# Projections on high and low halves, the modulation rows in the weights' ring, and one sequence for the fourth layer's attentions

## The chip, the cores and the metric

The kernel runs on one NeuronCore of a Trainium2 chip. The metric is the device time of one execution in microseconds (us). All data are float32; "fp32r" in a row is the matmul's reduced form of float32 operands.

## The reference

A sequence of 256 tokens of width 1024 goes through four layers. The first block has two layers (gated linear attention and a spatial gating unit, an output projection, cross attention to a memory, 16 experts in 4 groups); the second block has two layers with adaptive norms (the third: sparse "nsa" and block "moba" attention; the fourth: latent "mla" and sliding-window "swa" attention), each again with 16 experts. The adaptive norms take their scales, shifts and gates from a vector c:

```python
for layer in range(DEPTH):
    shift_m, scale_m, gate_m, shift_f, scale_f, gate_f = adaln(c, ada_w[layer], ada_b[layer])
    h = rmsnorm(x, norm_mix[layer]) * (1.0 + scale_m) + shift_m
    # even layer: nsa and moba; odd layer: mla and swa; both start from h @ w_in
    x = x + gate_m * mix.astype(x.dtype)
    h = rmsnorm(x, norm_ffn[layer]) * (1.0 + scale_f) + shift_f
    x = x + gate_f * grouped_moe_2(h, router_w, router_b, ...)
return rmsnorm(x, final_norm)
```

c times ada_w is 2 x 6144 numbers from 50 MB of weights; the projections and experts read 500 MB.

## The kernel before

**Weights.** All weights of the projections and experts come in pieces of 2 MB (128 x 4096) through `ring`, four slots. SyncE issues the loads in one order (L2210): load m waits on `halves_done`, which TensorE raises by two when it starts the piece after the one it gives back, and lands in slot m % 4. A first-block layer has 15 pieces before its experts (q with k, v, r, sv, u, xk0, xk1, out0, out1, xv0, xq0, xq1, xv1, xo0, xo1), the third layer 10, the fourth 6; the experts have 48 per layer.

**Projections.** `natural` keeps x stationary and moves 512 weight columns; `transposed` keeps 128 weight columns and moves x's 256 tokens. Both are plain float32 products of `product` (line 654 of every row: the helper `mm`); the profile shows a plain product as two TensorE records. x comes transposed (`turn`, L684), drained by ScalarE and VectorE in turn (`turned`, `modulated`, L1512, L1870).

**Experts.** The same ring, but each piece in halves: ScalarE writes the high part of a half to `hi_ring` (four half slots, L1155), VectorE writes what is left to `ring_parts` in the piece's place (L1494), and TensorE adds three products, high-high, high-low, low-high. One half later each half is given back. A branch after the loop (L873, L884) recomputes groups with more than 128 tokens; it runs in the third layer alone. Around the attention units the engines follow one list in a fixed order: scores, exponentials, transposed probabilities three steps apart.

**Modulation.** GpSimd loads the rows of ada_w, 48 loads of 1 MB, into `hi_ring` while that is free; VectorE multiplies each row with silu(c) and sums it (`modulation`, L1839, 96 rows) at places of the first two layers chosen by ADA_PLAN (3, 7, 1, 3, 7, 3 loads). GpSimd's next load waits on `ada_summed`.

**Order.** Each engine's stream is written out by hand. `first_layer` (TensorE, L902) runs q, k, alow, v, z, r, sv, rem, dec, u, kv, mix, xk0, o, xk1, turn0, out, xv0, turn1, xq, attention with xv1 in it, xo, turn2, router, experts. In the fourth layer TensorE runs c, the latents' norm and their up projection, mla's attention, then sq and sk, then swa's attention.

## Time and profile before

| | us |
|---|---|
| median of 3 runs (2514.18 to 2517.14) | 2515.72 |
| profiled execution | 2515.05 |
| its span | 2512.9 |
| projections of the second layer, first product to last add | 642.8 to 890.6 |
| experts of the second layer | 934.5 to 1245 |
| third layer: projections, then attention | 1270.7 to 1377.3, to 1458 |
| fourth layer: projections and attentions | 1994.6 to 2097.3 |
| TensorE, VectorE, ScalarE, GpSimd busy | 2192, 1504, 1084, 89 |

A timeline row gives the start of a run of like instructions, its length, engine, line, operation, output and input, shape and count; in brackets the idle time before it and what ended that. The granted clock of TensorE is a share of 2.4 GHz.

### The profile page before, as it was taken

The numbers are of one execution on the slowest core, as the hardware profiler recorded it, in microseconds if no ns is written. First come the engines' busy times: TensorE is split into PE (matmuls) and PEld (weight loads), VectorE is DVE, ScalarE is ACT, GpSimd is POOL, SyncE is SP. The second block draws the span as 40 slices with busy tenths as digits, with TensorE's granted clock in tenths as the row PEclk, the third lists the DMA queues.
The fourth block names the chain that finished last, engine by engine and source line by source line (L and its number), as shares of the span: only waits on it lengthen the run. The fifth ranks groups of instructions, "written<-read, shape, count | busy, mean of one in ns | idle before, by whom it ended". The sixth has DMA issues, their size and how long they took to land.

```text
span 2512.9 us, 25829 instructions
## 1 busy us (share of the span) xinstructions
...
## 2 busy tenths in 40 slices
...
GB/s 408 285 228 199 84 327 329 285 342 321 275 236 256 159 78 335 342 292 335 268 167 134 1 67 170 334 299 333 314 260 258 71 101 67 137 316 330 303 318 125
DMA packets 48680, 596.26 MB, mean 237 GB/s; under 512 B 5200, under 2 KB 7248, under 8 KB 8784
## 3 DMA queue, kind: packets, MB, share of 16 engines
...
## 4 chain that ended last, share of the span: by engine, by line
PE 64%; issue 21%; DVE 7%; ACT 3%; DMA 3%; POOL 1%; DVEq 0%; ACTq 0%; POOLq 0%
PE bank L654 58%; PE bank L684 2%; PE bank L873 2%; DMA hi_ring<-in_ada 1%; DMA x<-in_x_in 1%; PE bank L884 1%; DVE ring_parts L1494 1%; POOL small L2141 1%; DVE work L1494 1%; ACT hi_ring_parts L1155 1%; ACT mix L1155 0%; ACT work L1155 0%; DVE mix L1569 0%; DVE hi_ring L1839 0%; DVE work_parts L1494 0%
## 5 line engine op out<-in xcount | busy, mean ns | idle before, releaser
L1494 DVE TENSOR_TENSOR ring_parts<-ring,hi_ring_parts 128x2048 fp32r<-128x2048 f32 x384 | 860.6, 2285 | 112.8 <-ACT hi_ring_parts L1155 112.7
L1155 ACT ACTIVATE hi_ring_parts<-ring 128x2048 fp32r<-128x2048 f32 x384 | 722.7, 1913 | 144.3 <-PE bank L654 112.7
L654 PE MATMUL bank<-hi_ring_parts,xT_parts 128*128 128x512 f32 x1024 | 340.5, 405 | 48.6 <-DVE ring_parts L1494 48.6
L1155 ACT ACTIVATE work<-bank 128x512 f32<-128x512 f32 (+6 forms) x215 | 113.6, 531 | 612.3 <-PE bank L654 493.9
L654 PE MATMUL bank<-hi_ring_parts,work_parts 128*128 128x512 f32 x1024 | 328.5, 392 | 24.7 <-DVE work_parts L1494 24.7
L654 PE MATMUL bank<-hi_ring_parts,oT_parts 128*128 128x512 f32 x1024 | 331.3, 394 | 4.8 <-DVE ring_parts L1494 4.8
L654 PEld LDWEIGHTS bank<-hi_ring_parts,xT_parts 128*128 128x128 f32 x1024 | 199.1, 194 | 94.6 <-DVE ring_parts L1494 52.7
L654 PEld LDWEIGHTS bank<-hi_ring_parts,work_parts 128*128 128x128 f32 x1024 | 192.2, 188 | 69.9 <-issue 30.5
L654 PEld LDWEIGHTS bank<-hi_ring_parts,oT_parts 128*128 128x128 f32 x1024 | 192.3, 188 | 48.1 <-DVE ring_parts L1494 8.6
L654 PE MATMUL bank<-ring_parts,xT_parts 128*128 128x512 f32 x512 | 204.9, 400 | 0.0
L654 PE MATMUL bank<-ring_parts,oT_parts 128*128 128x512 f32 x512 | 199.5, 390 | 0.0
L654 PE MATMUL bank<-ring_parts,work_parts 128*128 128x512 f32 x512 | 199.5, 390 | 0.0
L1155 ACT ACTIVATE work_parts<-bank 128x512 fp32r<-128x512 f32 (+1 forms) x116 | 64.5, 560 | 251.7 <-PE bank L684 218.1
L654 PE MATMUL bank<-ring,oT 128*128 128x512 f32 x384 | 166.1, 593 | 4.6 <-DVE oT L1599 2.3
L654 PE MATMUL bank<-ring,xT 128*128 128x512 f32 (+3 forms) x480 | 162.9, 498 | 1.6 <-DVE xT L1870 1.6
L654 PE MATMUL bank<-xT,ring 128*128 128x256 f32 x656 | 148.2, 388 | 16.4 <-DMA xT<-in_xT_in 11.3
L654 PEld LDWEIGHTS bank<-xT,ring 128*128 128x128 f32 x656 | 127.2, 195 | 35.4 <-DMA xT<-in_xT_in 11.3
L654 PE MATMUL bank<-work 128*128 128x128 f32 (+4 forms) x712 | 119.6, 313 | 17.9 <-ACT work L1155 17.8
L654 PEld LDWEIGHTS bank<-ring,oT 128*128 128x128 f32 x384 | 72.5, 190 | 94.3 <-issue 94.3
L654 PEld LDWEIGHTS bank<-ring,xT 128*128 128x128 f32 x480 | 83.6, 190 | 76.4 <-issue 74.6
L1839 DVE CUSTOM_DVE_ANT_0 hi_ring<-hi_ring,silu_row 128x1024 f32<-128x1024 f32 x96 | 112.4, 1221 | 26.9 <-DMA hi_ring<-in_ada 25.7
L654 PEld LDWEIGHTS bank<-work 128*128 128x128 f32 (+1 forms) x712 | 104.1, 208 | 30.4 <-issue 19.3
...
## 6 DMA issues: line engine op xcount, KB each, us to landing
...
```

Source lines behind the costliest of these rows:

```text
L654: ins = nc.tensor.matmul(o, lhsT, rhs, start=start, stop=stop)
L684: ins = nc.tensor.transpose(bank[0:rows, c0:c1], src, ident[0:k, 0:k])
L873: ins = nc.tensor.matmul(psum[j][:, :], xg[0][:, c, :], w[:, c, :], start=c == 0, stop=c == DC - 1)
L884: ins = nc.tensor.matmul(psum[3 + n][:, :], ehT_plain[:, 0, j, :], w[:, j, n * 512:(n + 1) * 512], start=j == 0, stop=j == HC - 1)
L1155: return nc.scalar.activation(o, i, f, **kw)
L1494: return v.tensor_tensor(o, a, b, op)
L1839: v.tensor_tensor_reduce(out=here[:, r, :], in0=here[:, r, :], in1=silu_row, scale=1.0, scalar=0.0, op0=ALU.mult, op1=ALU.add, accum_out=s ...
L2141: nc.gpsimd.tensor_tensor(stat_out, stat_in, cs("half"), ALU.pow).then_inc(rstd_ready, 1)
```

## The change

Four things change. **Three passes:** all projections but xk0, xk1, xv0, xv1, e.ck, e.cv, o.up and the second block's out pieces are split like the experts' pieces and done as three fp32r passes per product; their x is split too (`first_x`, `second_x`, `first_o`, on ScalarE and VectorE, in place of one copy each). Each split stands at a fixed place in ScalarE's and VectorE's streams, and TensorE waits for both halves. **The modulation rows** become 24 pieces of 2 MB in the ring, at fixed places (FIRST_LAYER has nine, EVEN_LAYER six); their slots are given back by `ada_summed`. GpSimd loads none. Part of the sums moves to the third layer. **The gates' 24 columns** join piece e.kw. **Fourth layer:** sq and sk come before the latents' transposes, and mla and swa form one list of attention units. The low-rate product alow comes first in the second layer.

```diff
+FIRST_LAYER = ("q/ v/ a r/ a sv/ a a u/ xk0 xk1 out0/ out1/ a xv0 xq0/ xq1/ a xv1 xo0/ a xo1/ a a").split()
+EVEN_LAYER = "q/ c/ a kw/ a mq/ a ck a cv a mk/ a mv/ out0 out1".split()
+ODD_LAYER = "c/ sq/ sk/ up out0 out1".split()
+LINEAR = {"0": FIRST_LAYER, "1": FIRST_LAYER, "e": EVEN_LAYER, "o": ODD_LAYER}
...
+        class Part:
+
+
+            def __init__(self, name, h):
+                m, n = PIECE_AT[name]
+                self.slot, self.full = m % RING, 16 * (m // RING + 1)
+                self.n = n + h + 1
+                self.free = SPLIT_HALVES[self.n - 1 - HI_RING] + 1 if self.n > HI_RING else 0
+                self.raw = ring[:, self.slot, h * HALF:(h + 1) * HALF]
+                self.hi = hi_ring[:, (self.n - 1) % HI_RING, :]
+                self.lo = ring_parts[:, self.slot, h * HALF:(h + 1) * HALF]
+
...
+            def split_piece(name):
+
+                m, n = PIECE_AT[name]
+                assert PIECES[m] == ("pe", taken[0]), name
+                taken[0] += 1
+                pe.wait_ge(lo_ready, n + 2)
+                release[0] += owed[0]
+                owed[0] = 2
+                parts = [Part(name, h) for h in range(2)]
+                return [[side(p).rearrange("p (c n) -> p c n", c=DC // 2) for p in parts]
+                        for side in (lambda p: p.hi, lambda p: p.lo)]
+
             def mm(o, lhsT, rhs, start, stop):
...
+            def moving(x_, w, T, at, n):
+
+                hi, lo = (lambda c, k=k: w[k][c // 4][:, c % 4, at:at + n] for k in range(2))
+                t = slice(T * P, (T + 1) * P)
+                return [pair for c in range(DC) for pair in ((x_[0][:, c, t], hi(c)), (x_[0][:, c, t], lo(c)),
+                                                             (x_[1][:, c, t], hi(c)))]
+
+            def still(x_, w, m):
+
+                hi, lo = (lambda c, k=k: w[k][c // 4][:, c % 4, m * P:(m + 1) * P] for k in range(2))
+                return [pair for c in range(DC) for pair in ((hi(c), x_[0][:, c, :]), (lo(c), x_[0][:, c, :]),
+                                                             (hi(c), x_[1][:, c, :]))]
+
+            def natural3(name, w, T, x_, at=0, n=512):
...
+                tg = f"{l}"
+                parts = 4 * l
+
+                def low_rate():
+                    wl = pr("w_alow", 2, DC * 16)[:, l, :].rearrange("p (c n) -> p c n", c=DC)
+                    product(f"{tg}.alow", [(0, S, GATE_RANK, [(wl[:, c, :], plain_xT[:, c, :]) for c in range(DC)])])
+
+                if l:
                     for q in range(DC // 2):
                         ready(f"{l - 1}.turn3.{q}")
-                tg = f"{l}"
-                w = columns(piece())
-                transposed(f"{tg}.q", [lambda c, m=m: w[:, c, m * P:(m + 1) * P] for m in range(2)])
-                product(f"{tg}.k", [(T * 256, (T + 1) * 256, P, [(xT[:, c, T * P:(T + 1) * P], w[:, c, 256:512])
-                                                               for c in range(DC)]) for T in range(NT)])
+                    low_rate()
+                w = split_piece(f"{tg}.q")
+                for q in range(DC // 2):
+                    pe.wait_ge(parts_lo, parts + q + 1)
+                transposed3(f"{tg}.q", w, first_x, range(2))
+                both3(f"{tg}.k", w, first_x, 256)
                 if l == 0:
                     pe.wait_ge(setup_loaded, 32)
-                wl = pr("w_alow", 2, DC * 16)[:, l, :].rearrange("p (c n) -> p c n", c=DC)
-                product(f"{tg}.alow", [(0, S, GATE_RANK, [(wl[:, c, :], xT[:, c, :]) for c in range(DC)])])
-                w = columns(piece())
-                for T in range(NT):
-                    natural(f"{tg}.v.{T}", T, lambda c: w[:, c, :])
+                    low_rate()
+
+                def projected(n):
+                    w = split_piece(f"{tg}.{n}")
+                    for T in range(NT):
+                        natural3(f"{tg}.{n}.{T}", w, T, first_x)
+
+                projected("v")
 
                 def memory_values(q):
-                    w = columns(piece())
+                    w = columns(piece(f"{tg}.xv{q}"))
                     for T in range(NT):
...
             normed("o.turn0", 8)
-            w = columns(piece())
+            w = split_piece("o.c")
+            parts_ready(12)
             for T in range(NT):
-                natural(f"o.c.{T}", T, lambda c: w[:, c, 0:448], n=448)
+                natural3(f"o.c.{T}", w, T, second_x, n=448)
+            w = split_piece("o.sq")
+            for j in range(2):
+                transposed3(f"o.sq.{j}", w, second_x, (2 * j, 2 * j + 1))
+            w = split_piece("o.sk")
+            transposed3("o.sk", w, second_x, (0,))
+            both3("o.sv", w, second_x, 0)
             pe.wait_ge(lat_ready, 1)
...
+            attention(numbered(mla_units(), ATT["mla"]) + numbered(swa_units(), ATT["swa"]))
...
+            def split(name):
+
+                for h in range(2):
+                    part = Part(name, h)
+                    act.wait_ge(slot_full[part.slot], part.full)
+                    if part.free:
+                        act.wait_ge(halves_done, part.free)
+                    fn(part.hi, part.raw, ACT.Identity).then_inc(hi_ready, 1)
+
...
+            def x_hi(dest, src, q, tag=None):
+
+                if tag:
+                    banks.wait_drained(act, f"{tag}.{q}")
+                fn(dest[:, 2 * q:2 * q + 2, :], src[:, 2 * q:2 * q + 2, :], ACT.Identity).then_inc(parts_hi, 1)
+
...
-                    turned(f"{l - 1}.turn3")
+                    split(f"{tg}.q")
+                    turned(f"{l - 1}.turn3", plain_xT)
+                    for q in range(DC // 2):
+                        x_hi(first_x[0], plain_xT, q, f"{l - 1}.turn3")
+                split(f"{tg}.v")
+                if l:
+                    whole(alow[0:GATE_RANK, :], f"{tg}.alow")
                 whole(gqT, f"{tg}.q", scale=0.125)
-                whole(alow[0:GATE_RANK, :], f"{tg}.alow")
+                if l == 0:
+                    whole(alow[0:GATE_RANK, :], f"{tg}.alow")
+                split(f"{tg}.r")
                 for T in range(NT):
                     whole(gv[:, T, :], f"{tg}.v.{T}")
                 act.wait_ge(gla_abs, l + 1)
                 step(fn(gE, gE, ACT.Exp, scale=-1.0))
                 fn(gE, gE, ACT.Ln, bias=1.0).then_inc(gla_log, 1)
+                split(f"{tg}.sv")
                 for T in range(NT):
                     whole(gr[:, T, :], f"{tg}.r.{T}", ACT.Silu)
+                split(f"{tg}.u")
                 for T in range(NT):
                     whole(sv[:, T, :], f"{tg}.sv.{T}", ACT.Gelu_apprx_tanh)
                 whole(gE, f"{tg}.rem", ACT.Exp)
                 whole(decay, f"{tg}.dec", ACT.Exp)
+                split(f"{tg}.out0")
                 for T in range(NT):
                     whole(su[:, T, :], f"{tg}.u.{T}", ACT.Gelu_apprx_tanh)
                 for j in range(4):
                     whole(xkT[:, 2 * j:2 * j + 2, :], f"{tg}.xk.{j}")
-                for q in (0, 2):
-                    whole(oT[:, 2 * q:2 * q + 2, :], f"{tg}.turn0.{q}")
+                    if j == 1:
+                        split(f"{tg}.out1")
+                turned_hi(f"{tg}.turn0", first_o[0])
+                split(f"{tg}.xq0")
+                split(f"{tg}.xq1")
 
                 def memory_values(q):
                     for T in range(NT):
                         whole(xv[:, T, q * 512:(q + 1) * 512], f"{tg}.xv.{T}.{q}")
 
                 memory_values(0)
-                turned(f"{tg}.turn1")
+                turned_hi(f"{tg}.turn1", first_x[0])
                 for j in range(4):
                     whole(xqT[:, 2 * j:2 * j + 2, :], f"{tg}.xq.{j}", scale=0.0625)
-                attention(numbered(cross_units(f"{tg}.x"), ATT[f"{tg}.x"]), lambda: memory_values(1))
+                    if j == 1:
+                        split(f"{tg}.xo0")
+
+                def last_values():
+                    split(f"{tg}.xo1")
+                    memory_values(1)
+
+                attention(numbered(cross_units(f"{tg}.x"), ATT[f"{tg}.x"]), last_values)
                 if l == 0:
...
+            def modulation(pieces=1):
+
+                for _ in range(pieces):
+                    n = adas[0]
+                    adas[0] += 1
+                    m = PIECE_AT["a", n]
+                    dve.wait_ge(slot_full[m % RING], 16 * (m // RING + 1))
+                    rows = ring[:, m % RING, :].rearrange("p (r k) -> p r k", r=ADA_EACH)
                     for r in range(ADA_EACH):
-                        k = adas[0] - ADA_COLS * l
-                        adas[0] += 1
-                        v.tensor_tensor_reduce(out=here[:, r, :], in0=here[:, r, :], in1=silu_row, scale=1.0, scalar=0.0,
-                                               op0=ALU.mult, op1=ALU.add,
-                                               accum_out=sm("modc", 2, ADA_COLS)[:, l, k:k + 1]).then_inc(ada_summed, 1)
+                        k = n * ADA_EACH + r
+                        v.tensor_tensor_reduce(out=rows[:, r, :], in0=rows[:, r, :], in1=silu_row, scale=1.0, scalar=0.0,
+                                               op0=ALU.mult, op1=ALU.add, accum_out=sm("modc")[:, k:k + 1]) \
+                            .then_inc(ada_summed, 1)
...
-                    turned(f"{l - 1}.turn3")
+                    split(f"{tg}.q")
+                    turned(f"{l - 1}.turn3", plain_xT)
+                    x_lo(first_x, plain_xT)
+                split(f"{tg}.v")
                 p_ = bank(f"{tg}.k")
                 drained(f"{tg}.k", v.tensor_copy(gk, p_[:, :].rearrange("p (t n) -> p t n", t=2)))
-                modulation(l, ADA_PLAN["key"])
+                split(f"{tg}.r")
+                modulation()
 
                 p_ = bank(f"{tg}.z")
                 z = p_[:, :].rearrange("p (t n) -> p t n", t=2)
@@ -1925,7 +2130,9 @@
                 tell(gla_abs)
                 dve.wait_ge(gla_log, l + 1)
                 tt(gg, gg, gE, ALU.subtract).then_inc(gla_g, 1)
-                modulation(l, ADA_PLAN["gate"])
+                split(f"{tg}.sv")
+                modulation(3)
+                split(f"{tg}.u")
                 banks.wait_drained(dve, f"{tg}.rem")
                 for c in range(NCHUNK):
                     T = c // 2
@@ -1951,6 +2158,7 @@
                 tt(sv, sv, mixv[:, 2:3, :].broadcast_to([P, NT, 512]), ALU.add).then_inc(sgu_ready, 1)
                 dve.wait_ge(sgu_ready, l + 1)
 
+                split(f"{tg}.out0")
                 banks.wait_drained(dve, f"{tg}.dec")
...
-                turned(f"{tg}.turn0", oT)
-                residual(f"{tg}.out", l, ADA_PLAN["out"])
+                turned_lo(f"{tg}.turn0", first_o)
+                split(f"{tg}.out1")
+                residual(f"{tg}.out", l, (0, 1, 0, 0), f"{tg}.xq0")
                 layer_norm(x)
                 tell_x()
-                turned(f"{tg}.turn1")
-                modulation(l, ADA_PLAN["query"])
+                turned_lo(f"{tg}.turn1", first_x)
+                split(f"{tg}.xq1")
+                modulation()
+                split(f"{tg}.xo0")
                 attention(numbered(cross_units(f"{tg}.x"), ATT[f"{tg}.x"]))
-                residual(f"{tg}.xo", l, ADA_PLAN["xo"])
+                split(f"{tg}.xo1")
+                residual(f"{tg}.xo", l, (1, 1, 1, 0))
                 layer_norm(x)
                 tell_x()
                 turned(f"{tg}.turn2")
                 route(tg, "b_router", True)
                 step(v.tensor_scalar(mix[:, :, :], x[:, :, :], ALPHA, None, ALU.mult))
-                modulation_bias(l)
                 dve.wait_ge(rows_out, 128)
                 experts(f"{tg}.moe")
                 layer_norm(mix)
...
+            modulation_bias(0)
+            split("e.q")
+            adaptive_norm("e.turn0", 0, pr("norm_mix")[:, 0:8], 8, 0, second_x)
+
+            split("e.c")
+            modulation()
+            split("e.kw")
+            modulation()
             p_ = bank("e.c")
             for j, pos in enumerate(("pos_k", "pos_v")):
...
+            modulation_bias(1)
+            split("o.c")
+            adaptive_norm("o.turn0", 1, pr("norm_mix")[:, 8:16], 8, 0, second_x)
+            split("o.sq")
             banks.wait_drained(dve, "o.c.0")
             banks.wait_drained(dve, "o.c.1")
...
+            def freed(m):
+                kind, n = PIECES[m]
+                if kind == "pe":
+                    sp.wait_ge(halves_done, 2 * n + 2)
+                else:
+                    sp.wait_ge(ada_summed, ADA_EACH * (n + 1))
+
+            m = 0
+            for tag, linear in LINEAR.items():
+                for _ in range(len(linear) + RING):
+                    if m == 1:
+                        sp.wait_ge(xT_loaded, 16)
+                    if m == 2:
+                        sp.wait_ge(setup_loaded, 32)
+                    if m >= RING:
+                        freed(m - RING)
+                    load(m)
+                    m += 1
+                with sp.Fori(1, NMOE // RING) as g:
+                    for j in range(RING):
+                        sp.wait_ge(halves_done, g * (2 * RING) + (2 * (MOE_USER[tag] + j - RING) + 2))
```

## Rows read from the trace of the kernel before

**Rows 1.** The page: the chain that ended last, by engine.
```profile
PE 64%; issue 21%; DVE 7%; ACT 3%; DMA 3%; POOL 1%; DVEq 0%; ACTq 0%; POOLq 0%
```
**Rows 2.** Busy by stretch: start:end, us, PE, PEld, DVE, ACT, POOL, PEclk, DMA, GB/s.
```profile
642.80:890.60 247.80, 242.48 (x864) 151.37 (x864) 112.65 (x209) 32.67 (x57) 21.01 (x25) 1.00 0.61 239
934.50:1245.00 310.50, 298.06 (x1397) 246.95 (x1398) 251.38 (x160) 210.89 (x157) 0.00 (x0) 0.99 0.86 325
```
**Rows 3.** TensorE's timeline, second layer: start, length, what, count, idle before.
```profile
704.58 13.98 PE L654 MATMUL bank<-ring,xT 128*128 128x512 f32 x32
...
723.63 13.98 PE L654 MATMUL bank<-work,ring 128*128 128x256 f32 x64
...
757.78 27.70 PE L654 MATMUL bank<-ring,oT 128*128 128x512 f32 x64 [1.16 <-DVE oT L1512]
...
862.05 27.71 PE L654 MATMUL bank<-ring,oT 128*128 128x512 f32 x64 [1.16 <-DVE oT L1599]
```
**Rows 4.** VectorE's timeline, second layer.
```profile
639.39 0.07 DVE L1491 MEMSET small<- 128x1 f32 x2
...
889.86 0.69 DVE L1553 SCALAR_TENSOR_TENSOR x<-x,bank 128x512 f32<-128x512 f32 x1 [6.25 <-PE bank L654]
```
**Rows 5.** The chain of waits, experts of the second layer: start, length, matmuls.
```profile
1045.18 16.37 PE bank L654 x72
```
**Rows 6.** TensorE's timeline, third layer.
```profile
1270.72 24.41 PE L654 MATMUL bank<-xT,ring 128*128 128x256 f32 x112 [1.60 <-DVE xT L1870]
1294.97 3.73 PE L654 MATMUL bank<-ring,xT 128*128 128x128 f32 x32
...
1305.57 3.65 PE L654 MATMUL bank<-params,xT 128*128 128x24 f32 x32
...
1363.39 13.90 PE L654 MATMUL bank<-ring,xT 128*128 128x512 f32 x32
```
**Rows 7.** Groups by line and shape: busy us, mean ns, idle before and releaser.
```profile
L1494 DVE TENSOR_TENSOR ring_parts<-ring,hi_ring_parts 128x2048 fp32r<-128x2048 f32 x384 | 860.6, 2285 | 112.8 <-ACT hi_ring_parts L1155 112.7
L1155 ACT ACTIVATE hi_ring_parts<-ring 128x2048 fp32r<-128x2048 f32 x384 | 722.7, 1913 | 144.3 <-PE bank L654 112.7 <-DMA ring<-in_weights 31.2
...
L654 PEld LDWEIGHTS bank<-hi_ring_parts,work_parts 128*128 128x128 f32 x1024 | 192.2, 188 | 69.9 <-issue 30.5
...
L1839 DVE CUSTOM_DVE_ANT_0 hi_ring<-hi_ring,silu_row 128x1024 f32<-128x1024 f32 x96 | 112.4, 1221 | 26.9 <-DMA hi_ring<-in_ada 25.7
```
**Rows 8.** The ring's loads in the third layer's projections, from issue to landing.
```profile
DMA to landing us min/median/max: 7.6/7.7/8.9
```
**Rows 9.** Busy by stretch, start of the kernel (columns of Rows 2).
```profile
28.00:45.00 17.00, 17.00 (x49) 7.47 (x48) 2.45 (x5) 4.94 (x7) 2.12 (x4) 1.00 1.01 425
```
**Rows 10.** Busy by stretch, after a wait in the first layer.
```profile
98.50:102.00 3.50, 3.46 (x16) 3.47 (x17) 3.33 (x7) 0.00 (x0) 0.00 (x0) 0.50 0.00 0
```
**Rows 11.** TensorE's timeline, first layer.
```profile
31.58 14.00 PE L654 MATMUL bank<-ring,xT 128*128 128x512 f32 x32
...
98.54 3.75 PE L654 MATMUL bank<-work,params 128*128 128x128 f32 x16 [5.29 <-DVE work L1494]
102.11 13.99 PE L654 MATMUL bank<-work,ring 128*128 128x256 f32 x64
```
**Rows 12.** ScalarE's timeline, start of the kernel.
```profile
33.39 1.06 ACT L1155 ACTIVATE silu_row<-silu_row 128x1024 f32<-128x1024 f32 x1 [2.81 <-DMA silu_row<-in_vecs]
```
**Rows 13.** TensorE's timeline, fourth layer.
```profile
1994.58 12.27 PE L654 MATMUL bank<-ring,xT 128*128 128x448 f32 x32 [1.60 <-DVE xT L1870]
2014.02 1.54 PE L684 MATMUL bank<-consts,work 128*128 128x128 f32 x6 [7.18 <-DVE work L2064]
...
2032.96 5.95 PE L654 MATMUL bank<-work 128*128 128x128 f32 x24 [0.88 <-ACT work L1155]
...
2074.42 0.44 PE L684 MATMUL bank<-consts,work 128*128 128x128 f32 x2 [2.29 <-DVE work L1494]
...
2097.33 2.02 PE L654 MATMUL bank<-consts,small 128*128 128x128 f32 x16 [1.08 <-DVE oT L1599]
```

402 lines of the change are left out of this document (225 added, 177 removed).

## The prediction

> **What bounds the kernel now.** I read the page's chain first: TensorE carries 64% of it [rows 1]. Then the stages. In the second layer's projections TensorE is busy 242.5 of 247.8 us at full granted clock, in its experts 298 of 310.5 us, with VectorE at 251 and ScalarE at 211 [rows 2]. The expert loop is the same code after the change; only its beginning differs. So the change acts in four stretches: the projections of the two first-block layers, of the third and of the fourth. There TensorE is the bound, the other engines have room on average, and what must be walked is the order in which splits, loads and sums now queue. Before, TensorE's timeline has nearly no gap: u starts at 704.58, xk0 at 723.63, out at 757.78, xo at 862.05 [rows 3], and the last residual add of VectorE is at 889.86 [rows 4].
>
> **Prices on TensorE.** Plain: 32 records of 512 columns take 13.98 us [rows 3]; two records make one product, so 0.865 us per 512 columns and 13.9 us per piece. Three passes: 72 in 16.37 us [rows 5], 0.227 each, 0.68 per 512 columns, 10.9 us per piece: 3.0 us less. That holds for v, r, sv, u, out0, out1, xo0, xo1 (two layers) and e.mv: 17 pieces, 50 us; o.c (448 columns) gives 2.6. The other split pieces move 256 columns per pass. Plain: 112 records in 24.41 us [rows 6], 0.218, so 0.436 a product. No row shows a high-or-low pass of 256 columns. Nearest is the plain 128-column product: a record loads 128x128 weights and streams 256 cycles' worth, 32 in 3.73 us, 0.117 [rows 6]. A 512-column pass takes 0.01 us more than half a plain record (0.227 against 0.217), so between 0.117 and 0.127 I take 0.122. Bounds: 0.107 (256 columns at 2.4 GHz) below; 0.19, the mean of one weight load in the experts [rows 7], above, if it were not overlapped. Three passes then cost 0.366 against 0.436: 2.2 us per full piece (q, xq0, xq1 twice; e.q, mq, mk; o.sq): 22 us. Three value products (e.vs, e.vw, o.sv) grow from 128 to 256 columns: 16 each from 0.234 to 0.366, +6; the gates' own product (3.65 us [rows 6]) goes. In all TensorE has about 50 + 3 + 22 + 3 (small tiles) - 6 + 4 = 76 us less to do.
>
> The Trainium skill (TensorE: Matmul & The Clock Gate, LDWEIGHTS) states that a weight load takes the columns divided by 1.2 in ns, 107 ns for 128. By that rule a 256-column pass would stand at its lower bound and the 1224 such passes would take some 16 us less than at 0.122; the row of 0.117 lies between, so the sum stays with the row.
>
> **Prices of what is added.** ScalarE's high half 1.91 us, VectorE's low half 2.29 [rows 7]: 3.8 and 4.6 us per piece, and 1.9 + 2 x 2.3 = 6.5 us from a landed piece to both halves ready. 31 pieces. A sum over the modulation rows is as before, 96 of them, 112.4 us busy [rows 7] or 1.17 each, 4.6 per 2 MB piece. A load lands 7.6 us after its issue when alone [rows 8]; a second right behind it about 5 us later (2.1 MB at the 425 GB/s of a full queue [rows 9]). Load m waits for piece m-4; with sum pieces in between, four slots hold only about two TensorE pieces. A PE wait has a second price: after 5.29 us of idleness the 16 records at 98.54 ran at granted clock 0.50 (1.2 GHz) [rows 10, 11]; that is up to 2 us per stall of 3 us or more; I take 2, bounds 0 and 2.
>
> **Second layer, walked on the clock of before.** VectorE ends the norm at 639.4 [rows 4] and now does split q (to 644.0) before it may copy turn3; the copies end 645.4, the four hi/lo pairs of x (a quarter of a split's width, 0.5 and 0.6 us and up [rows 7]) at 648.2. TensorE runs alow first, from 645.5, partly at the low clock, to 651.0. q 651.0 to 662.7, v to 673.6, z to 674.7, r from 674.7 (plain: 675.3).
> - sv's load waits for v's release, which comes with r's first matmul: issue 674.7, lands 682.3, halves ready 688.8; r ends 685.6. Stall 3.3.
> - VectorE then sums a1 to 693.4; only that frees u's slot. u lands about 702 behind a3; VectorE sums a2, a3 to 702.7; u's halves are ready 708.5. sv and two small products end 703.5: stall 5. u starts 708.6 against 704.58.
> - Behind split u on VectorE stand (each as long as before) gkd, the gate statistics, POOL's power and 5.5 us of scaling: 725.3, so xk0 starts 727.2 against 723.63 [rows 3]: **+3.5**.
> - o and xk1 unchanged; turn0 at 758.4; high then low part in place of a copy: out at 762.3 against 757.78, **+4.5**. out takes 21.8 for 27.7. xv0 is plain; x returns in time (split xq0 delays the last residual by 1.6, hidden by xv0). xq starts 801.9, ends 825.3 (before 830.0).
> - In the attention ScalarE stops at split xo1: its load goes out with xv1's first matmul (831.2), second in the queue, lands 844.1, high halves end 847.9, then xv1's two drains; the pipeline resumes 1.5 us, not 5, ahead of before. xo starts 861.2 against 862.05.
> - xo takes 21.8; VectorE has split xo1 and three sums between its adds and ends at 885.8, 2 us behind TensorE, against 890.55 [rows 4]: **-4.7**.
> - The experts' second piece waits for xo1, which is released only when the experts' first matmul runs (before, it waited for a piece four earlier and was there). It lands 7.6 later, its first half is ready after 1.9 + 2.3 more, 11.9 us; the first piece lasts 7 us (its first 4 us at the low clock). Stall 4.8 and 2 us of low clock: **+6.5**, in both first-block layers. It is hidden by nothing: the loop's chain is TensorE's.
> Sum of the layer: **+1.8**.
>
> The Trainium skill (same page, Architectural detail) says that ScalarE and VectorE are strictly first in, first out. Here that is what makes a split in front of a drain cost more than its 3.8 us; the walk above already has it.
>
> **First layer.** v was at 31.58 [rows 11]. Now split v stands on ScalarE behind the silu at 33.39 to 34.45 [rows 12], so v starts at 41.1, after an idle TensorE; the same chain sv, a1, u then gives u at 88.6 and xk0 at 107.2 against 102.11 [rows 11]: +5.1. From there as in the second layer, -8.2 to the last add and +6.5: **+3.4**. Gained here: the modulation rows no longer share the full queue [rows 9]; the walk has that in the 7.6 us loads.
>
> **Third layer** [rows 6]. split e.q stands before the norm: +4.6; hi and lo of x: +2.4. q starts 1277.8 against 1270.72 (partly low clock), ends 1291.5; c ends 1306.0; kw 1314.7. mq's load waits for c's release (1306.0), halves ready 1320.2: stall 5.5. ck from 1333.9; cv from 1345.5; mk's load waits for ck's release: ready 1359.6, mk from 1360.3; mv's load goes out there, ready 1374.4, mk ends 1372. mv ends about 1385.6 against 1377.3: **+8.3**. The attention behind it is as before.
>
> **Fourth layer** [rows 13]. c starts 7.1 later (2001.7; bounds 4.6 to 9), ends 2013.3. sq and sk (11.7 + 8.8 us) now run while VectorE norms the latents, where TensorE waited 7.18 us. cqT at 2033.8, mla's scores at 2048.6 against 2032.96. Before, mla took 15.3 us, the projections 21, swa 27.2. As one sequence the three steps of drain and fill between them go: from 2032.96 to mla's last transposes 12.9, 2.3 to swa's first, which stand at 2074.42, then 22.9 to 2097.33: 38.1. End 2086.7 against 2097.33: **-10.6** (bounds -6 to -15).
>
> **Sum.** +3.4 + 1.8 + 8.3 - 10.6 = +2.9 us. The profiled execution took 2515.05 (span 2512.9), 0.7 under the median of 2515.72; on the median that is **2518.6**. The 76 us that TensorE saves are spent on loads that come too late for the split, on splits in front of other work, and on the starts of the experts. About 0.2% (5 us) is what a measurement can tell from no change.
>
> **Rivals.**
> - *The queues bite less* (chance 0.28). If sv's and u's stalls, the low clock behind stalls and half of the third layer's waits fall away (loads two deep land sooner, sums done earlier), each first-block layer gives back 10 and the third 12: 2518.6 - 32 = 2486. For it: TensorE's sum alone gives -76. Against: the 7.6 us and 6.5 us are firm rows and r lasts 10.9.
> - *More of them* (0.17). VectorE's order (split, sums, drains) makes waits that I have not walked, above all at turn1 and in the first layer's start, where DMA is full [rows 9]: 5 to 10 us a layer more, 2540.
> - *The weight load bounds the 256-column pass* (0.10): 1224 passes, at 0.19 they cost 0.068 each more, 83 us, some 75 on the path: 2594. It decides from 0.145 per pass, where three passes equal two records. For it: a load's own row lasts 0.19; against: plain 128-column records follow each other at 0.117 with the same load.
> - *The walk holds* (0.45), within 2506 to 2530 by the bounds of clock, x parts and merged attention; of this 0.10 below 2510.7, 0.25 within 0.2%, 0.10 above 2520.8.
> Faster 0.28 + 0.10 = 0.38; same 0.25; slower 0.10 + 0.17 + 0.10 = 0.37. Range 2479 to 2550: it leaves out the load-bound case and the outer tails of the first two.
>
> **What would show it.** Right: 256-column passes 0.12 us apart; q of the second layer some 8 us later after the norm; sv and u begun after waits of 3 and 5 us for VectorE's low half; ScalarE waiting about 13 us for xo1's load inside the cross attention; a wait of about 5 us before the experts' second piece, in the first two layers alone; the third layer's projections about 8 us longer, the fourth's about 10 shorter; expert loops else unchanged. Wrong: passes at 0.15 or more; sv and u without wait; or a changed branch for overfull expert groups, which here runs in the third layer and would follow the routing if rounding moved a token.

## The result, and the profile of the changed kernel

The changed kernel takes 2549.6 us (median of 4 runs, 2545.8 to 2552.6) against 2516.4 of the kernel before on the same chip: ratio 1.0133, interval 1.0118 to 1.0148. It is slower by 33 us. The forecast was 2518.6, no change; it is missed by 31 us. The value still lies in the stated range of 2479 to 2550, by 0.4 us at its end, and that is luck: the range was wide because the rivals pointed both ways, while the kernel is slower by a measured 33 us for a reason that is not in the forecast's sum.

A clock for the comparison are the norms of VectorE, which stand in both kernels at the same points: a 2.47 us statistic behind each layer's output projection, behind the cross attention, and behind the experts; in the third and fourth layers the sum of squares of x. In VectorE's timeline of the changed kernel (start, duration, engine, line, operation, result<-operands, count, what ended the wait):

```profile
180.06 2.47 DVE L1710 BATCH_NORM_STATS2 small<-x 128x6 f32<-128x512 f32 x4
...
644.76 2.47 DVE L1710 BATCH_NORM_STATS2 small<-mix 128x6 f32<-128x512 f32 x4 [1.52 <-DVEq L2021]
...
914.87 2.47 DVE L1710 BATCH_NORM_STATS2 small<-x 128x6 f32<-128x512 f32 x4
...
1279.54 2.47 DVE L1710 BATCH_NORM_STATS2 small<-mix 128x6 f32<-128x512 f32 x4 [1.28 <-DVEq L2021]
...
2020.51 4.49 DVE L1655 TENSOR_TENSOR ring_parts<-ring,hi_ring_parts 128x2048 fp32r<-128x2048 f32 x2
2024.91 1.22 DVE L2050 CUSTOM_DVE_ANT_0 mix<-x 128x1024 f32<-128x1024 f32 x1
...
2158.53 1.22 DVE L2050 CUSTOM_DVE_ANT_0 mix<-x 128x1024 f32<-128x1024 f32 x1
```

Stretch by stretch, read from such rows of every kernel's profiled execution (us; "to out" is up to the norm behind the output projection, "to xo" on to the norm before the experts, "experts" on to the norm behind them; the third layer from there to its second sum of squares; the fourth from its first to its second, with the 4.6 us of the early split in front of the first counted in where there is one):

| kernel | 1st: to out | to xo | experts | 2nd: to out | to xo | experts | 3rd | 4th |
|---|---|---|---|---|---|---|---|---|
| before | 164.8 | 104.3 | 361.0 | 156.6 | 103.9 | 357.9 | 240.9 | 146.7 |
| changed | 180.1 | 99.3 | 365.4 | 169.9 | 100.2 | 364.7 | 249.3 | 138.2 |
| no sums | 155.7 | 97.2 | 360.2 | 146.9 | 97.2 | 360.0 | | |
| out0's split later | 178.1 | 99.4 | 365.5 | 165.5 | 98.4 | 365.5 | 251.5 | 143.4 |
| slots freed at the end | 168.3 | 93.6 | 358.3 | 161.3 | 95.6 | 357.4 | 247.5 | 143.5 |
| + both splits later | 172.9 | 94.0 | 357.8 | 161.7 | 95.5 | 359.7 | 248.8 | 143.4 |
| + rows later | 163.4 | 94.1 | 359.9 | 151.8 | 95.9 | 359.7 | 248.8 | 143.5 |
| first two plain | 156.7 | 104.3 | 360.7 | 156.3 | 104.3 | 357.7 | 248.3 | 143.4 |
| mixed forms | 159.6 | 93.6 | 359.2 | 163.9 | 93.7 | 359.4 | 241.5 | 143.4 |

So in the changed kernel's profiled execution the first layer is 14.7 us longer than before, the second 16.4, the third 8.3 longer and the fourth 8.5 shorter; that is 30.9, and the two profiled executions differ by 30.7 (2545.8 and 2515.1 us). One of these numbers is not typical. The fourth layer's projections and attention are the same code in the changed kernel and in ten of the experiments, but took 138.2 us there and 141.9 to 143.5 in them. The windows over TensorE's last part of it (window, length, busy us and instructions of each engine, granted clock, DMA share, GB/s), first the changed kernel, then the one of experiment 1:

```profile
2087.00:2122.00 35.00, 25.39 (x148) 21.71 (x148) 24.03 (x114) 18.83 (x65) 0.00 (x0) 0.90 0.00 1
2122.00:2159.00 37.00, 32.64 (x105) 16.68 (x104) 9.28 (x17) 1.62 (x5) 0.00 (x0) 1.00 0.31 114
```
```profile
2043.00:2080.00 37.00, 27.16 (x147) 23.25 (x148) 24.00 (x114) 18.57 (x64) 0.00 (x0) 0.85 0.04 18
2080.00:2118.00 38.00, 34.52 (x106) 18.33 (x106) 8.82 (x17) 1.95 (x6) 0.00 (x0) 0.96 0.18 60
```

The same instructions, a granted clock of 0.90 and 1.00 against 0.85 and 0.96. The median of the changed kernel is 3.8 us above its profiled execution, which fits a fourth layer that is as a rule 3 to 5 us shorter than before, not 8.5. A difference of 5 us in this layer between two single profiles is therefore no result.

The profile's page of the changed kernel says who is late. The splits, in the groups of the costliest instructions (busy us, mean ns | idle time just before them and what ended it):

```profile
L1655 DVE TENSOR_TENSOR ring_parts<-ring,hi_ring_parts 128x2048 fp32r<-128x2048 f32 x446 | 999.3, 2284 | 248.3 <-ACT hi_ring_parts L1243 248.0
L1243 ACT ACTIVATE hi_ring_parts<-ring 128x2048 fp32r<-128x2048 f32 x446 | 839.2, 1912 | 389.6 <-DMA ring<-in_weights 249.8
```

A split costs what it cost before [rows 7], but ScalarE now waits 249.8 us for loads in front of splits (31.2 before [rows 7]), and VectorE behind it. TensorE's busy time fell from 2192 to 2143 us, and its share of the chain that ends last from 64% [rows 1] to 58%; the mean granted clock fell too, from 0.936 to 0.926 in the profiled executions.

In the second layer the passes are what the forecast said (TensorE's timeline; the third number of a row is its duration, the starts give the pitch):

```profile
666.92 0.28 PE L713 MATMUL bank<-xT_parts,hi_ring_parts 128*128 128x256 f32 x1
667.04 0.28 PE L713 MATMUL bank<-xT_parts,ring_parts 128*128 128x256 f32 x1
667.16 0.28 PE L713 MATMUL bank<-mix_parts,hi_ring_parts 128*128 128x256 f32 x1
...
678.84 0.39 PE L713 MATMUL bank<-hi_ring_parts,mix_parts 128*128 128x512 f32 x1
679.06 0.39 PE L713 MATMUL bank<-hi_ring_parts,xT_parts 128*128 128x512 f32 x1
```

At full granted clock (1.00 from 666 to 684) a pass of 256 columns follows the last every 0.120 us, one of 512 every 0.227. What was not in the forecast comes behind u. The chain of waits in that stretch (start, us, what), and below it SyncE's issues and ScalarE's rows:

```profile
718.29 5.81 issue
725.74 17.39 DMA ring<-in_weights
748.92 33.03 PE bank L713 x144
783.16 2.49 DVE work_parts L1655 x4
786.01 37.38 PE bank L713 x128
```
```profile
704.39 4.34 SPq L2408 DMA_DIRECT2D ring<-in_weights  x2
724.89 1.28 SPq L2408 DMA_DIRECT2D ring<-in_weights  x3
...
743.16 3.71 ACT L1243 ACTIVATE hi_ring_parts<-ring 128x2048 fp32r<-128x2048 f32 x2 [17.52 <-DMA ring<-in_weights]
746.88 1.28 ACT L1243 ACT_TABLE_LOAD   x1
748.18 1.09 ACT L1243 ACTIVATE work<-bank 128x512 f32<-128x512 f32 x2
```

At 724.89, behind u's first product (724.10), SyncE issues three loads at once: xk0, xk1 and out0. Only xk0 had waited for sv's slot; the slots of the other two, held by sums, had been free since 717.5 at the latest, but their loads stood behind xk0's in SyncE's program. out0 is the third and lands 17.4 us later. ScalarE waits 17.5 us for it and makes out0's high halves (743.16) in front of the two drains of u (748.18), which free the PSUM bank that xk0 needs, so xk0 starts at 748.9. The forecast had it at 727.2 plus the 14.7 of the layer before, 741.9.

And at the start of the experts:

```profile
956.59 0.79 PE L713 MATMUL bank<-hi_ring_parts,xT_parts 128*128 128x512 f32 x1 [7.38 <-DVE ring_parts L1655]
957.61 1.05 PE L713 MATMUL bank<-hi_ring_parts,xT_parts 128*128 128x512 f32 x2
...
969.65 0.80 PE L713 MATMUL bank<-hi_ring_parts,xT_parts 128*128 128x512 f32 x1 [5.46 <-DVE ring_parts L1655]
970.67 1.05 PE L713 MATMUL bank<-hi_ring_parts,xT_parts 128*128 128x512 f32 x2
```

The second piece waits 5.5 us, and behind the wait TensorE runs at its lower clock once more (rows of 1.05 us for two passes where 0.62 is usual; the granted clock of 969.6 to 980 is 0.78). The wait was forecast at 4.8, the low clock at 2.

### The profile page after: what moved, and what is told of

The parts are those of the page before. It is cut to its first block, busy times and chain, and to the rows that moved or that the text cites. A ratio compares the mean times of both kernels' runs of the same rounds, so it can differ in the third digit from the quotient of the medians.

```text
span 2544.0 us, 27291 instructions
## 1 busy us (share of the span) xinstructions
PE 2143.4 (84%) x10128; PEld 1724.8 (68%) x10128; DVE 1653.3 (65%) x2020; ACT 1213.3 (48%) x1258; POOL 65.4 (3%) x34
## 4 chain that ended last, share of the span: by engine, by line
PE 58%; issue 22%; DVE 8%; DMA 6%; ACT 4%; POOL 1%; DVEq 0%; POOLq 0%; SPq 0%; ACTq 0%
PE bank L713 52%; DMA ring<-in_weights 4%; PE bank L960 2%; PE bank L743 2%; DVE ring_parts L1655 2%; ACT hi_ring_parts L1243 1%; POOL small L2365 1%; PE bank L971 1%; DVE work L1655 1%; ACT work L1243 1%; DMA consts<-in_cst 1%; DVE work_parts L1655 1%; DMA hi_ring<-in_weights 1%; ACT mix L1243 0%; DMA silu_row<-in_vecs 0%
## 5 line engine op out<-in xcount | busy, mean ns | idle before, releaser
L1655 DVE TENSOR_TENSOR ring_parts<-ring,hi_ring_parts 128x2048 fp32r<-128x2048 f32 x446 | 999.3, 2284 | 248.3 <-ACT hi_ring_parts L1243 248.0
L1243 ACT ACTIVATE hi_ring_parts<-ring 128x2048 fp32r<-128x2048 f32 x446 | 839.2, 1912 | 389.6 <-DMA ring<-in_weights 249.8
L713 PE MATMUL bank<-hi_ring_parts,xT_parts 128*128 128x512 f32 (+2 forms) x1264 | 436.5, 404 | 80.3 <-DVE ring_parts L1655 62.1
L713 PEld LDWEIGHTS bank<-hi_ring_parts,xT_parts 128*128 128x128 f32 x1264 | 250.4, 198 | 137.2 <-DVE ring_parts L1655 64.0
L713 PE MATMUL bank<-ring_parts,xT_parts 128*128 128x512 f32 (+1 forms) x672 | 270.1, 402 | 0.0
L1243 ACT ACTIVATE work<-bank 128x512 f32<-128x512 f32 (+7 forms) x213 | 111.2, 529 | 317.0 <-PE bank L713 197.6
L713 PEld LDWEIGHTS bank<-ring_parts,xT_parts 128*128 128x128 f32 x672 | 134.3, 200 | 26.2
L713 PEld LDWEIGHTS bank<-ring_parts,oT_parts 128*128 128x128 f32 x640 | 121.0, 189 | 24.0
L713 PE MATMUL bank<-work 128*128 128x128 f32 (+3 forms) x680 | 113.9, 313 | 23.8 <-ACT work L1243 23.8
L2036 DVE CUSTOM_DVE_ANT_0 ring<-ring,silu_row 128x1024 f32<-128x1024 f32 x96 | 111.5, 1220 | 29.8 <-DMA ring<-in_weights 29.7
L713 PE MATMUL bank<-xT_parts,hi_ring_parts 128*128 128x256 f32 x328 | 98.1, 299 | 24.4 <-DVE mix_parts L1655 24.4
```

Source lines behind the costliest of these rows:

```text
L713: ins = nc.tensor.matmul(o, lhsT, rhs, start=start, stop=stop)
L1243: return nc.scalar.activation(o, i, f, **kw)
L1655: return v.tensor_tensor(o, a, b, op)
L2036: v.tensor_tensor_reduce(out=rows[:, r, :], in0=rows[:, r, :], in1=silu_row, scale=1.0, scalar=0.0, op0=ALU.mult, op1=ALU.add, accum_out=s ...
```

## Experiments

The stretches of most of them are in the table above; they come from one profiled execution each. All but the fourth start from the changed kernel; the diffs are cut to their core. Ratios are to the kernel before, run again beside each group of experiments (medians 2514.5, 2515.4, 2515.0 and 2514.8).

**1. The slots are freed at the end of a piece.**

```
- sp.wait_ge(halves_done, 2 * n + 2)     # told with the NEXT piece's first product
+ banks.wait_full(sp, LAST[m])           # told by the piece's own last product; the experts' pieces as before
```

> A slot of the ring is given back when the last product of its piece has ended, not with the first product of the next piece; all else is as in the changed kernel. In its second layer, sv's product ended at 718.3 but u's first one came at 725.7, and the loads of xk0, xk1 and out0 stood behind that release; out0 landed at 743. Theory 'order of the loads' (the loads that the queue holds behind a late release, and the splits that then stand in front of other work, make the missed time): out0 lands some 8 us earlier and the stretch up to the first-block output projection shortens by 6 to 9 us in each of the first two layers; the experts' second piece, held by xo1, no longer waits (5 us and some low clock, 7 in all, per layer). Together about 28 us off 2549.6: 2521. Rival 'the splits' own work' (ScalarE and VectorE simply have too much in front of the drains, whenever the data comes): only the experts' 14 us go, 2536. Rival 'the rows' (sum pieces in the ring): u still waits for its slot, held by a sum, so little more than the experts' 14 us, 2533.

Measured: 2504.8 us, ratio to before 0.9965 (0.9953 to 0.9978): 45 us less than the changed kernel (42 by the two ratios, 41 between the profiled executions), more than any theory gave, and 0.35% faster than before. Each stretch of the first two layers gave something: 11.7 and 8.6 to out, 5.7 and 4.6 to xo, 7.1 and 7.3 in the experts. In the second layer:

```profile
693.67 1.28 SPq L2415 DMA_DIRECT2D ring<-in_weights  x3
...
711.89 3.71 ACT L1250 ACTIVATE hi_ring_parts<-ring 128x2048 fp32r<-128x2048 f32 x2 [11.65 <-DMA ring<-in_weights]
...
717.66 31.33 PE bank L720 x144
...
920.64 15.62 PE bank L720 x60
```

The same three loads go out right at sv's end (693.67; u's first product came at 698.7). The third still lands 17.4 us later, but ScalarE waits 11.7 us in place of 17.5; xk0 starts 97.5 us behind the layer's norm in place of 104.2. The experts run through their first two pieces (60 passes, then on) without a wait. In the cross attention ScalarE's stop for xo1's load falls from 11.4 to 4.0 us and is gone from the chain. So the loads behind a late release are the cause of most of the loss; the rival that only the experts' 14 us would go falls. The rival of the rows falls as an account of the whole, but not as a part of it: xk0 still starts 4 us later than before, and experiments 3 and 7 show why.

**2. out0's split later.** ScalarE splits out0 behind u's drains and two of xk's (and out1 behind the other two), VectorE behind the gating products.

```
- split(out0); whole(su ...); whole(xkT ..., 0 and 1); split(out1); whole(xkT ..., 2 and 3)     # ScalarE
+ whole(su ...); whole(xkT ..., 0 and 1); split(out0); whole(xkT ..., 2 and 3); split(out1)
- split(out0); states ...; gating products ...                                                  # VectorE
+ states ...; gating products ...; split(out0)
```

> Only the place of one split changes: ScalarE makes out0's high halves after the drains of u and of xk's first piece, VectorE its low halves after the states and the gating products; all loads and rows as in the changed kernel. Theory 'order': in the changed kernel TensorE stood from 737 to 749 because ScalarE waited for out0's load (landed 743.2) in front of u's drains; with the drains in front xk0 starts about 9 to 11 us earlier in each of the first two layers. Of this 6 to 9 us reach the output projection, since out0's own halves are ready only by about 755: in all 12 to 18 us off 2549.6, 2535. Rival 'the splits' own work': the 8.4 us that the two engines need for out0 only move to a later place in front of xk's drains and the copies, which delays them as much: no change, 2549.

Measured: 2542.5 us. 7 us less than the changed kernel, 1.9 and 4.4 of it in the stretches to out. Half of the theory's 12 to 18, so neither it nor the rival holds alone: xk0 starts 97.9 us behind the layer's norm in place of 104.2, but the copies of the o products, which come later on VectorE, only 118.8 in place of 120.9. Experiments 5 and 6 say why.

**3. No sums.**

```
- "q/ v/ a r/ a sv/ a a u/ xk0 xk1 out0/ out1/ a xv0 xq0/ xq1/ a xv1 xo0/ a xo1/ a a"
+ "q/ v/ r/ sv/ u/ xk0 xk1 out0/ out1/ xv0 xq0/ xq1/ xv1 xo0/ xo1/"               # and no modulation()
```

> Leaves out the 96 sums over the modulation rows and their 24 loads (the third and fourth layers are then modulated by the bias alone, so their routing and the time from 1280 us on is not comparable). The ring carries only TensorE's pieces. Read over the first two layers, which need no rows: the stretch from the start to the norm behind the second layer's experts took 1248.5 us before and 1279.5 after the change. Theory 'the rows make the loads late': four slots then hold four TensorE pieces, all splits come early, the stalls at sv, u, out0, xo0, xo1 and at the experts' second piece go, and TensorE's 31 us per layer are gained less some 9 us of start: the stretch ends near 1279.5 - 2 x 37 = 1205. Rival 'the splits' own work': only the two experts' stalls (14 us) and little else go: 1262. Between these, the sums' own 56 us on VectorE per layer have little to do with it.

Measured over the two layers: 1217.1 us up to the third layer's norm, against 1279.5 in the changed kernel and 1248.5 before. Nearer to the first theory (1205) than to the rival (1262). The later layers of this kernel lack their modulation and are not compared. The chain of the second layer runs from the norm to xk0 without a load (its last line begins with the 16 records of the spatial unit's mix; xk0 follows at 700.12, below it from TensorE's timeline):

```profile
628.41 52.10 PE bank L712 x260
...
695.69 1.24 DVE work L1654
696.95 1.24 DVE work L1654
698.23 33.15 PE bank L712 x160
```
```profile
700.12 13.98 PE L712 MATMUL bank<-work,ring 128*128 128x256 f32 x64
```

These mix products start 85.2 us behind the norm and xk0 itself 87.1 (at 700.12; 97.5 in experiment 1, 93.6 before). The loads in this kernel are still told by the next piece's product; with four slots for TensorE's pieces alone that lateness is covered. This kernel leaves out the sums' time on VectorE together with their slots; experiment 7 keeps all sums.

**4. The fourth layer's order alone**, in the kernel before: sq and sk (plain) moved behind c, their queries kept in `silu_row`.

```
- attention(mla); sq, sk products; attention(swa)
+ c; sq, sk products; latents, up ...; attention(mla + swa)
```

> The kernel before with only the fourth layer's order changed: the pieces sq and sk are projected right behind c, plain, and both attentions run as one sequence. Theory 'the fourth layer's order is a gain of its own': TensorE no longer waits 7.2 us for the latents' norm, and the drains and fills between mla, the projections and the second attention go, 38.1 us in place of 64.4 less 3 longer plain projections: 10 to 13 us less than before, about 2505. Rival 'the gain of that layer came from three passes and early splits': under 4 us, 2512.

Measured: 2505.5 us, ratio 0.9968 (0.9957 to 0.9979), 9 us faster than before. The fourth layer takes 137.2 us (1978.84 to 2116.03) against 146.7:

```profile
1978.84 1.23 DVE L1851 CUSTOM_DVE_ANT_0 mix<-x 128x1024 f32<-128x1024 f32 x1
...
2116.03 1.22 DVE L1851 CUSTOM_DVE_ANT_0 mix<-x 128x1024 f32<-128x1024 f32 x1
```

9.5 us, a little under the expected 10 to 13. With the same order and three passes besides, the layer takes 141.9 to 143.5 (138.2 in the changed kernel's own execution). There c starts 6.2 us later than here, counted from the end of the experts, and mla's scores 4.6 to 6.5 later. From these scores to the last transposes the merged attention takes 43.8 us here, about 43.5 in experiments 2, 6, 10 and 11, and 40.1 (2087.4 to 2127.5) in the changed kernel's own execution.

**5 and 6. Freed at the end and out0's split later**, in two forms: out1's split of ScalarE in front of the first turn, then behind it. The second, on ScalarE:

```
- split(out0); whole(su ...)
+ whole(su ...)
  for j in range(4): whole(xkT ..., j); if j == 1: split(out1 -> out0)
  turned_hi(turn0)
+ split(out1)
```

> The slots freed at the last product, and out0's split behind the drains of u and of xk's first piece. With the slots freed early, out0 lands at 711.9 in the second layer and ScalarE's split still stands in front of u's drains: xk0 starts at 717.7, where sgu's rows would let it start about 708. Theory 'order': xk0 starts 7 to 9 us earlier in each of the first two layers and out0's halves are long ready when the output projection begins, so nearly all of it arrives: 14 to 18 us off 2504.8, 2489. Rival 'the splits' own work': as in the run with the split moved alone (1.9 and 4.4 us), most is lost again behind the later split: 6 us, 2499.

> Repeats the run with slots freed at the last product and out0's split behind the drains, which came out 13 us slower than with the slots alone, but with one line put elsewhere: ScalarE's split of out1 now stands behind the first turn's high halves, not in front of them. Theory: in that run xk0 did start 2.4 us earlier after the norm (95.1 us against 97.5), no more, because sgu's rows on VectorE (behind u's late load) come last; what it lost was out1's split in front of the turn, 3.7 us on the path in both layers, and its knock-on at the output projection. So now 4 to 5 us off 2504.8: 2500. Rival 'every split placed later is a loss on VectorE's side': 2515 again.

Measured: 2518.0 and 2511.4 us, both slower than experiment 1 alone (2504.8). Both expectations of a gain failed. VectorE's timeline in the second form:

```profile
738.20 4.49 DVE L1662 TENSOR_TENSOR ring_parts<-ring,hi_ring_parts 128x2048 fp32r<-128x2048 f32 x2 [9.71 <-ACT hi_ring_parts L1250]
742.61 2.85 DVE L2202 COPY mix<-bank 64x512 f32<-64x512 f32 x4
```

VectorE waits 9.7 us for a split that ScalarE makes only behind xk's drains, then works on it 4.5 us, and the copies of the o products, which lead through a norm to the first turn, begin 118.0 us behind the layer's norm; in experiment 1 they began at 112.5 (732.68). And nothing is won in front of it: xk0 starts 97.1 us behind the norm, 97.5 in experiment 1, because the spatial unit's rows on VectorE come last there. So the place behind the gating products is not free on VectorE: a split there stands on the chain. In experiment 2 the same took back part of the gain. The first form differs from the second by out1's split alone and is 6.7 us slower (5.8 by the ratios). "The splits' own work" is right for this one place.

**7. The rows later.** On top of the second form; two sums are made behind the gating rows and the gating products.

```
- "q/ v/ a r/ a sv/ a a u/ xk0 xk1 out0/ out1/ ..."
+ "q/ v/ a r/ sv/ a u/ a a xk0 xk1 out0/ out1/ ..."
```

> The kernel of the line above with another order of the ring in the first two layers: the four sum pieces among the first block's are placed so that neither sv's nor u's load waits for a slot that a sum still holds (sv takes q's slot, u that of an old sum), and two of the sums are made behind the gating rows and the gating products instead of in front of u. Theory 'a sum that holds a slot makes u late, and u's low halves hold up sgu's chain': without any sum xk0 starts 85.2 us after the norm, with them 97.5; now it should start near 86 and the stretch from norm to norm shorten by 10 to 12 us in the second layer and by as much in the first: 22 us off, 2478. Rival 'the sums only move': two sums (9 us) in front of the states and the copies delay the o products and the first turn by as much: 2498.

Measured: 2493.7 us, ratio 0.9913 (0.9896 to 0.9929), 17.7 less than its base (22 expected; the 2478 had counted on a base of 2500). It is the fastest kernel here with three passes everywhere. The stretches to out fell by 9.5 and 9.9 us:

```profile
632.74 50.63 PE bank L720 x260
...
701.08 15.88 PE bank L720 x80
```
```profile
702.97 13.98 PE L720 MATMUL bank<-work,ring 128*128 128x256 f32 x64
```

TensorE now goes from q to sv's end without a stop; the mix products start 83.7 us behind the norm and xk0 85.6 (at 702.97; 97.1 in its base). All sums are still made, so it was not their time. The stalls at sv and u, which the forecast had priced at 3.3 and 5 us, came from the slots that sums take up: sv's load stood behind v's release, because sums held the places between, and u's behind a sum. For u the edit moves two sums out of VectorE's way as well, and how much is slot and how much is VectorE's order isn't shown. With out0's split in the place of experiment 1 this order of the rows was not run.

**8. The first two layers plain**, slots freed at the end, rows still in the ring.

```
+ "q v a r a sv a a u xk0 xk1 out0 out1 a xv0 xq0 xq1 a xv1 xo0 a xo1 a a"         # all drains as before
```

> As the run with slots freed at the last product, but every piece of the first two layers is a plain product, as before; the modulation rows stay in the ring, the third and fourth layers are those of the changed kernel. It prices the three passes of these layers with the ring as it is. Theory 'the net gain of three passes there is small': the stretches return to those of the kernel before, 269 + 361 + 260.5 + 358 = 1248 against 1234: 14 us on 2504.8, 2518. Rival 'the rows in the ring were the harm': the plain kernel would suffer from late loads too and stand above 2530.

Measured: 2509.6 us (2518 expected), ratio 0.9973 (0.9964 to 0.9983). No stall is left in either projection stretch:

```profile
11.21 114.02 PE bank L720 x400
...
634.36 112.07 PE bank L720 x400
```

In the second layer the times are those of before to 0.4 us. In the first, the stretch to out is 8.1 us shorter than before: before, the chain of that stretch ran through the modulation rows, whose first loads took 25 us in a full queue [rows 9] in front of VectorE's work. The kernel before:

```profile
31.74 1.06 POOL hi_ring L2152 x2
32.80 25.38 DMA hi_ring<-in_ada
58.20 1.22 DVE hi_ring L1839
```

So with plain products and the early release the rows in the ring are a gain, and the rival that puts this kernel above 2530 falls; their harm shows only together with the splits. Plain products with the late release were not run. Up to the third layer's norm: 1248.5 before, 1239.9 here, 1234.5 with three passes and slots freed at the end, 1279.5 with three passes as changed.

**9. The first block plain**, slots freed at the end.

```
- "q/ v/ a r/ a sv/ a a u/ xk0 xk1 out0/ ..."
+ "q v a r a sv a a u xk0 xk1 out0/ ..."       # no halves of these five, nor of x
```

> As the run with slots freed at the last product, but the pieces q, v, r, sv and u of the first two layers are plain products again (x is used whole, no halves of x or of these five pieces are made); out, xq and xo stay three passes. Theory 'in the first block the three passes cost more than they save': from the first instruction to the norm behind the output projection 168.3 us passed (before: 164.8), in the second layer 161.3 (before: 156.6), while out's passes alone save 6; plain, the stretches should take 159 and 151: 20 us off 2504.8, 2485. Rival 'the three passes save TensorE's time there': 5 pieces x 2.8 us x 2 layers come back, 28 us longer less the start's 8 per layer: 2517.

Measured: 2505.1 us, the same as with all of them split; both the theory (2485) and its rival (2517) missed. In the second layer out0's load, third in its queue, goes out at 691.8 and lands at 708.4, ScalarE waits 14.9 us for it in front of u's drains, and xk0 starts 98.7 us behind the norm (97.5 in experiment 1): there, what the plain pieces gain or lose is overwritten by that wait. In the first layer the stretch to out is 5.3 us shorter than in experiment 1, in the second 2.9 longer.

**10. The third layer plain**, slots freed at the end.

```
- "q/ c/ a kw/ a mq/ a ck a cv a mk/ a mv/ out0 out1"
+ "q c a kw a mq a ck a cv a mk a mv out0 out1"
```

> As the run with slots freed at the last product, but all pieces of the third layer are plain. Theory (the walk of the third layer, +8.3 measured and predicted): the start (split of e.q and the halves of x in front of q) and the waits for mq's and mv's halves go; 8 to 10 us off 2504.8, 2496. Rival 'without late releases the third layer's passes pay': no change or slower by up to 10, 2510.

Measured: 2496.9 us, ratio 0.9927 (0.9910 to 0.9943), 8 less, as expected. Its stretch falls from 247.5 to 241.6 (5.9 us; the rest is within what single executions differ).

**11 and 12. Mixed forms.** Three passes for out, xq and xo alone; then for xq and xo alone. Both with slots freed at the end, the third layer plain, the last sum of each layer behind the last turn.

```
+ "q v a r a sv a a u xk0 xk1 out0/ out1/ a xv0 xq0/ xq1/ a xv1 xo0/ a xo1/ a a"   # 11, out0's split as in 6
+ "q v a r a sv a a u xk0 xk1 out0 out1 a xv0 xq0/ xq1/ a xv1 xo0/ a xo1/ a a"     # 12
- residual(xo, ..., (1, 1, 1, 0))
+ residual(xo, ..., (1, 1, 0, 0)); ...; turned(turn2); modulation()
```

> Three passes only where their pieces come early: in the first two layers out, xq and xo (q, v, r, sv, u plain), in the third layer none; slots freed at the last product, the splits of out0 and out1 behind the drains and the turn, the last sum of each layer behind the last turn instead of in front of the last add. Theory: with all pieces plain the first stretch took 156.7 and 156.3 us without a stall, out's passes save 6 of that (150.5 each, against 163.0 and 164.2 with out0's split in the way of u's drains); the stretch to the next norm 94 less 2; the third layer 8 less: 2505.1 - 13 - 14 - 4 - 8 = 2466. Rival 'out0's load, third in its queue, still holds the chain': 2485.

> As the run of mixed forms, but out is plain too: in the first two layers only xq and xo are three passes, in the third none; the rest (slots freed at the last product, the last sum behind the last turn, the fourth layer as changed) stays. It prices out's three passes. Theory 'out's passes save 6 us of TensorE and lose as much and more on the way' (its split in front of the copies and the first turn, low halves of the turned rows in place of a copy, two more waits): from norm to norm the first stretch took 164 in the second layer with out as three passes, 156.3 all plain; the second stretch 93.7 with xq and xo as three passes; after a plain out it may be 3 longer, since xv0 no longer covers the norm in full. So 4 to 5 us less per layer than 2487.3: 2478. Rival 'out's passes do pay': 12 us more, 2499.

Measured: 2487.3 (ratio 0.9887, 0.9870 to 0.9903) and 2487.6 us (0.9881, 0.9863 to 0.9900). Both are 1.1 to 1.2% faster than before, the best of the study, and both missed what was expected (2466 and 2478). In the first the stretches to out took 159.6 and 163.9 in place of 150.5, with out0's split in the same place as in experiment 6: in the second layer VectorE waits 10.7 us for its high halves (to 724.92), works on it, and the copies of the o products begin 116.9 us behind the norm, 110.9 with out plain. With out plain they took 157.2 and 159.7, the norm of the third layer came 7.7 us earlier (1221.7 against 1229.4, 8 expected) and the profiled execution ended 5.4 us earlier; the medians don't show it. Whether out's three passes cost the 5 us or nothing stays open; the rival that they pay, 12 us, falls. What does pay is the pair xq and xo: the stretch to xo takes 93.6 to 96.3 us in these two kernels, 93.6 and 95.6 in experiment 1, where the sums stood as in the changed kernel, and 104.3 with all plain. In the last kernel the chain of the second layer's end is TensorE and one add:

```profile
843.04 22.04 PE bank L720 x96
865.17 0.70 DVE x L1730
```

where experiment 1 had the load of the last sum in front of the last adds, 863.19 with 7.73 us.

## Where the prediction was right and where it was wrong, step by step

The number kept within its range by luck, as said above; what follows goes by the terms of the sum, +3.4, +1.8, +8.3 and -10.6 for the four layers. Measured in the profiled execution: +14.7, +16.4, +8.3 and -8.5. The first two carry 26 of the 28 us missed there.

**Right: the prices.** The 256-column pass was taken at 0.122 us and runs at 0.120; the rival of a weight load that bounds it at 0.19 falls, and the sum's bound below, 0.107, is not reached either. (By the rule of the Trainium skill, TensorE: Matmul & The Clock Gate, LDWEIGHTS, a weight load of 128 columns takes 107 ns, and a pass would have stood at that bound; the measured pitch is 12% above it.) One product was reckoned wrong, without weight for the sum: 1224 passes at 0.015 us are 18 us, not 16. 512 columns took 0.227. A split costs 3.8 and 4.6 us a piece. A lone load landed after 7.5 to 7.8 us.

**Right: the steps that were walked, up to u.** Shifted by the 14.7 us of the first layer, sv was forecast at 703.6 and began at 703.9, u at 723.3 and began at 724.1, behind waits of 3.7 and 5.8 us (3.3 and 5 forecast); in the first layer v was forecast at 41.1 and began at 41.0, u at 88.6 and came at 89.1.

**Right: third layer.** +8.3 forecast, 249.3 against 240.9 measured, +8.3, with mq's and mv's waits where they were put (5.8 and 1.6 us, 5.5 and 2.4 forecast). Experiment 10 takes them away.

**Half right: fourth layer.** -10.6 forecast, -8.5 in the profiled execution, -3.2 to -4.8 in the ten experiments with the same code. The merged order is worth 9.5 alone (experiment 4). Two terms were mis-sized. c was set 7.1 us late and is 6.2 late, but what was to be made good behind it is not: mla's scores come 4.6 to 6.5 us later than with plain products in the same order. And the merged attention, 38.1 us in the sum, takes 40.1 in the changed kernel's own execution and 43.5 to 43.8 in experiments 2, 4, 6, 10 and 11.

**Right: the experts' start.** +6.5 forecast; the experts' stretches are 4.4 and 6.8 us longer than before, and experiment 1 takes 7.1 and 7.3 off them. In the first layer a part is hidden by other differences of the stretch.

**Wrong: the step "Behind split u on VectorE ... so xk0 starts 727.2" and the one before it.** The walk gave a load 7.6 us, or about 5 more for a second one right behind it, and asked only whether its own slot was free. It left out that SyncE issues loads in the stream's order: out0's slot was free, but its load stood behind xk0's, which waited for sv's release, and that release is told by u's first product, not by sv's end. So three loads went out together and the third took 17.4 us; the prediction's own prices give 17.6 for a third (7.6 and twice 5), so the price was right, and it was never applied to this load. The walk also had no line for split out0 at all, though it stands in front of u's drains on ScalarE. Cost in the second layer: 7.0 us at xk0 (748.9 against 741.9), 9.0 at out (786.0 against 762.3 + 14.7 = 777.0); in the first layer xk0 came at 113.2 against 107.2, 6.0 late. Experiment 1 gives 6.7 of it back in the second layer by telling the release earlier, experiment 7 brings xk0 to 85.6 us behind the norm against 104.2.

**Wrong: the step "x returns in time" and the attention.** xq began at 827.4 against 816.6 forecast (1.8 more), xo at 889.3 against 875.9 (2.6 more), the norm came at 914.9 against 890.6 - 4.7 + 14.7 = 900.6 (0.9 more). The cause is the same, loads behind a late release: ScalarE split xo0 from 848.6 on, in front of two drains of xq, and xo1 from 872.3 on, where the walk had the load landed at 844.1 + 14.7 = 858.8. With the slots freed at the end the two stretches to xo shrink by 5.7 and 4.6.

**Wrong: a gain set to nothing.** "Gained here: the modulation rows no longer share the full queue; the walk has that". It had not: with plain products experiment 8 shows 8.1 us of gain in the first layer from the rows' place. (It also has the early release, which changes nothing in its second layer.) So three passes and late loads cost that layer 23 us, not 15.

**The forecast's own rival.** "More of them" (0.17) is what happened: waits not walked, 11 and 15 us more than the sum in two layers, instead of 5 to 10 a layer. It was looked for at turn1 and in the first layer's start; it was at out0. "The queues bite less" was the opposite of this kernel, but experiment 7 is its picture: 2494 with three passes everywhere and most of the late loads gone, 8 us above its 2486.
